# Moving 512 columns by bank halves in conv-in and the first MLP's up units, with the sums on GpSimd

## The reference, cut to what matters

```
mod = silu(c) @ ada_w[i] + ada_b[i]; sh1, sc1, gt1, sh2, sc2, gt2 = split(mod, 6)
h = modulate(rmsnorm(x, norm_g[0, 0]), sh1, sc1)
b_gate, c_gate, hv = split(h @ w_in, 3)          # w_in: 1024 x 3072, "conv-in"
x = x + gt1 * ((b_gate * causal_conv3(c_gate * hv)) @ w_out)
h = modulate(rmsnorm(x, norm_g[0, 1]), sh2, sc2)
x = x + gt2 * (square(relu(h @ w1)) @ w2)        # w1: 1024 x 4096 "up", w2 "down"
```

## Time and profile before

| what | us |
|---|---|
| median of 3 runs | 1351.02 (1350.86 to 1354.01) |
| span of the profiled execution, first to last instruction | 1350.7 |
| PE, DVE, ACT, POOL busy in the span | 1303.9, 948.4, 701.1, 128.3 |
| conv-in's units on PE | some 36 to 114 |
| first MLP on PE | some 141.5 to 332 |

### The profile page before, as it was taken

One profiled execution on the slowest core, in us unless ns is written; L12 is line 12 of the kernel. 1 busy time (PEld: TensorE's weight loads), 2 busy tenths in 40 slices (PEclk: granted clock), 3 DMA queues, 4 the chain that ended last, 5 costly groups with the idle time before them and its releaser, 6 DMA issues. The chain is left out here.

```text
span 1350.7 us, 24951 instructions
## 1 busy us (share of the span) xinstructions
PE 1303.9 (97%) x10507; PEld 1130.7 (84%) x10507; DVE 948.4 (70%) x1433; ACT 701.1 (52%) x1211; POOL 128.3 (9%) x133
## 2 busy tenths in 40 slices
PE   4999999999999999999999999999999999999997
PEld 2998888997899887788888887888888998888886
DVE  1887788976768776685556888666657677756655
ACT  2534544434467455564444648654445566644443
POOL 0000000010200864100000142000000021000000
PEclk9999999999999999999999999999999999999999
DMA  9997899995341012356665532465565544565561
GB/s 363 373 366 236 302 350 381 356 344 161 110 156 64 4 35 97 98 178 196 188 192 177 176 121 74 150 203 192 187 196 160 170 143 126 172 188 192 183 197 51
DMA packets 177559, 256.90 MB, mean 190 GB/s; under 512 B 10472, under 2 KB 122536, under 8 KB 177448
## 3 DMA queue, kind: packets, MB, share of 16 engines
q1 hardware_dynamic: 177448, 255.31, 57.0%
HBM read 254.25 MB, written 1.05 MB: 189 GB/s over the span
## 5 line engine op out<-in xcount | busy, mean ns | idle before, releaser
L1507 DVE TENSOR_TENSOR w_lo<-stage,w_hi 128x1024 fp32r<-128x1024 f32 (+1 forms) x372 | 447.3, 1238 | 160.4 <-ACT w_hi L882 160.0
L882 ACT ACTIVATE w_hi<-stage 128x1024 fp32r<-128x1024 f32 (+1 forms) x378 | 379.9, 1049 | 211.7 <-PE acc L2311 191.9
L2309 PE MATMUL acc<-w_hi,z_hi 128*128 128x512 f32 x640 | 252.7, 395 | 1.6 <-DVE z_lo L1956 1.6
L2311 PE MATMUL acc<-w_hi,z_lo 128*128 128x512 f32 x640 | 249.4, 390 | 0.0
L2310 PE MATMUL acc<-w_lo,z_hi 128*128 128x512 f32 x640 | 249.2, 389 | 0.0
L2252 PE MATMUL un<-h_both,w_hi 128*128 128x256 f32 x736 | 214.9, 292 | 1.8 <-POOL w_lo L853 1.1
L2253 PE MATMUL un<-h_both,w_hi 128*128 128x256 f32 x736 | 208.8, 284 | 0.0
L2254 PE MATMUL un<-h_both,w_lo 128*128 128x256 f32 x736 | 208.8, 284 | 0.0
L2252 PEld LDWEIGHTS un<-h_both,w_hi 128*128 128x128 f32 x736 | 141.6, 192 | 9.5 <-issue 5.4
L2309 PEld LDWEIGHTS acc<-w_hi,z_hi 128*128 128x128 f32 x640 | 120.1, 188 | 27.8 <-issue 3.9
L2253 PEld LDWEIGHTS un<-h_both,w_hi 128*128 128x128 f32 x736 | 141.7, 193 | 1.2 <-issue 0.7
(11 more groups left out here) (393 smaller groups left out, 1885.1 us busy)
## 6 DMA issues: line engine op xcount, KB each, us to landing
stage<-in_mlp_w SPq DMA_DIRECT2D x64, 1024.0 KB
ada_buf<-in_ada_w SPq DMA_DIRECT2D x48, 1024.0 KB, 11.1
stage<-in_w_up SPq DMA_DIRECT2D x32, 1024.0 KB
stage<-in_w_down SPq DMA_DIRECT2D x32, 1024.0 KB
stage<-in_conv_w_in SPq DMA_DIRECT2D x12, 1024.0 KB
stage<-in_rw_w_rkv SPq DMA_DIRECT2D x12, 1024.0 KB
stage<-in_w_in_a SPq DMA_DIRECT2D x8, 1024.0 KB
stage<-in_w_kv_b SPq DMA_DIRECT2D x8, 1024.0 KB
```

Of the source, the lines that this page charges most:

```text
L882: A_(w_hi[u % 2][:, half, 0:n], stage[u % NSTAGE][:, half, 0:n], ACT.Copy).then_inc(hi_made, 1)
L1507: V.tensor_tensor(w_lo[u % 2][:, half, 0:n], stage[u % NSTAGE][:, half, 0:n], w_hi[u % 2][:, half, 0:n].bitcast(F32), ALU.subtract).then_i ...
L2309: MM(y, z_hi[:, kt, q], wh[:, i, :], start=(first and kt == 0), stop=False, skip_group_check=True)
L2311: ins = MM(y, z_lo[:, kt, q], wh[:, i, :], start=False, stop=(last and kt == KT - 1), skip_group_check=True)
```

## The change

Conv-in's 12 units and the first MLP's 16 up units (`HALF_UNITS`) are made by `half_unit`: W_hi moves both parts of h, 512 columns, and W_lo moves h_hi, 256 columns. The first output half goes to bank un[0] in full, then the second to bank un[1]. Each bank then holds two partial results side by side. ACT copies each bank as it stands to an SBUF tile `halves`; POOL adds the two parts. In the MLP POOL also makes the maximum with 0 and the product zf. DVE no longer makes the square; in conv-in it takes the last four sums from SBUF in place of PSUM. ACT's copy of the next unit's first half is queued behind z_hi. The lora_mu products move behind POOL's last three squares, `halves` takes the place of sq, one gate row moves to the place of the middle constants, and their load is queued behind SP's wait for x. Some waits are rewritten as links.

```diff
+        HALF_UNITS = [*range(U_CONV_IN, U_CONV_IN + 12), *(U_MLP[0] + 2 * UPD * g + j for g in range(GROUPS) for j in range(UPD))]
@@ SP
                 if u == U_MLP[0] + 8:
+                    sp.wait_ge(sem("x_ready"), x_done(N_MLP0))
                     sp.dma_start(const[1][:], A["const_table"][:, CONST_AT[1]:CONST_AT[2]]).then_inc(sem("const_mid_in"), 16)
-                    sp.wait_ge(sem("x_ready"), x_done(N_MLP0))
@@ POOL
+            for i in range(len(HALF_UNITS)):
+                pool.wait_ge(un_free, freed(half_use(i)))
+                both = halves[i % 2]
...
+                if i < 12:
+                    G.tensor_tensor(to, both[:, :, 0, :], both[:, :, 1, :], ALU.add).then_inc(sum_made, 1)
+                else:
+                    k = Z_MLP0 + i - 12
+                    link(G.tensor_tensor(to, both[:, :, 0, :], both[:, :, 1, :], ALU.add))
+                    link(G.tensor_scalar(both[:, :, 1, :], to, 0.0, None, ALU.max))
+                    pool.wait_ge(z_lo_made, k - 1)
+                    G.tensor_tensor(zf[k % 2][:], both[:, :, 1, :], to, ALU.mult).then_inc(zf_ready, 1)
+                if i >= len(HALF_UNITS) - 3:
+                    lora_scale(*LORA_COLS[i - len(HALF_UNITS)])
@@ ACT
+            def copy_half(i, m):
+                if m:
+                    act.wait_ge(unit_done, HALF_UNITS[i] + 1)
+                else:
+                    act.wait_ge(half_done, i + 1)
+                if 2 <= i < 14:
+                    act.wait_ge(sum_made, i - 1)
+                A_(halves[i % 2][:, m, :, :], un[m][:, :, :], ACT.Copy).then_inc(un_free if m else half_free, 1)
@@ ACT, mlp
-                            A_(relu_b[j % 2][:], un[(v + j) % 2][:], ACT.Relu).then_inc(relu_ready, 1)
+                            if j == 0:
+                                copy_half(12 + UPD * g, 0)
+                            copy_half(12 + UPD * g + j, 1)
...
                         if m == 0:
+                            if j < UPD - 1:
+                                copy_half(12 + UPD * g + j + 1, 0)
                             copy_set(COPIED_AT.get(S_MLP + 2 * UPD * g + j))
@@ DVE, mlp
-                            V.scalar_tensor_tensor(out=zf[k % 2][:], in0=un[(v + j) % 2][:], scalar=0.0, in1=relu_b[j % 2][:],
-                                                   op0=ALU.max, op1=ALU.mult).then_inc(zf_ready, 1)
@@ DVE, conv
-                    V.tensor_tensor(u_pad[:, t0:t0 + 2, 2:PADT], un[(V_CONV + j) % 2][:], tmp[:, t0:t0 + 2, :], ALU.mult).then_inc(un_free, 1)
+                    link(V.tensor_tensor(u_pad[:, t0:t0 + 2, 2:PADT], halves[j % 2][:, :, 0, :], tmp[:, t0:t0 + 2, :], ALU.mult))
@@ PE
+            def half_unit(i, ready=None):
+                def rows(kt, m):
+                    MM(un[m][:, :, :], wh[:, kt, c], h_both[:, kt, :, :], start=(kt == 0), stop=False, skip_group_check=True)
+                    ins = MM(un[m][:, 0, :], wl[:, kt, c], h_hi[:, kt, :], start=False, stop=(kt == KT - 1), skip_group_check=True)
...
+                together = KT - 2 if ready is not None else 0
+                if i:
+                    pe.wait_ge(half_free, i)
...
+                for m in range(2):
+                    if m:
+                        pe.wait_ge(un_free, freed(half_use(i) - 1))
+                    for kt in range(together, KT):
...
+                        rows(kt, m)
```

More of the change, by code:

```diff
@@ L202, in build @@
         zf = [at(f"zf{i}", [P, 2, SEQ], scr_off + 12 * 1024 + 2048 * i) for i in range(2)]
-        relu_b = [at(f"relu{i}", [P, 2, SEQ], scr_off + 16 * 1024 + 2048 * i) for i in range(2)]
+        halves = [at(f"halves{i}", [P, 2, 2, SEQ], sq_off + 4096 * i) for i in range(2)]
         up_sum = [at(f"up_sum{i}", [P, 2, SEQ], scr_off + 16 * 1024 + 2048 * i) for i in range(2)]
@@ L2278, in unit, with low_parts @@
                     ins.then_inc(unit_done, 1)
+            def half_unit(i, ready=None):
+                u = HALF_UNITS[i]
+                wh, wl = w_hi[u % 2], w_lo[u % 2]
+                def rows(kt, m):
+                    c = slice(P * m, P * m + P)
+                    MM(un[m][:, :, :], wh[:, kt, c], h_both[:, kt, :, :], start=(kt == 0), stop=False, skip_group_check=True)
+                    ins = MM(un[m][:, 0, :], wl[:, kt, c], h_hi[:, kt, :], start=False, stop=(kt == KT - 1), skip_group_check=True)
+                    if kt == KT - 1:
+                        ins.then_inc(unit_done if m else half_done, 1)
+                def low_parts(kt):
+                    if kt % (KT // 2) == 0:
+                        pe.wait_ge(lo_made, 2 * u + kt // (KT // 2) + 1)
+                together = KT - 2 if ready is not None else 0
+                if i:
+                    pe.wait_ge(half_free, i)
+                if together:
+                    pe.wait_ge(un_free, freed(half_use(i) - 1))
+                for kt in range(together):
+                    low_parts(kt)
+                    ready(kt)
+                    for m in range(2):
+                        rows(kt, m)
+                for m in range(2):
+                    if m:
+                        pe.wait_ge(un_free, freed(half_use(i) - 1))
+                    for kt in range(together, KT):
+                        if m == 0:
+                            low_parts(kt)
+                            if ready is not None:
+                                ready(kt)
+                        rows(kt, m)
             def up_unit(u, pair, ready=None):
@@ L2463, in mlp @@
                         if m == 0:
-                            free_bank(v + UPD * g + j)
-                            unit(u + 2 * UPD * g + j, un[(v + j) % 2], (h_hi, h_lo), ready)
+                            half_unit(12 + UPD * g + j, ready)
                             ada_piece(S_MLP + 2 * UPD * g + j)
@@ L2500, in _ @@
             for j in range(12):
-                free_bank(V_CONV + j)
-                unit(U_CONV_IN + j, un[(V_CONV + j) % 2], (h_hi, h_lo), h_ready(N_CONV) if j == 0 else None)
+                half_unit(j, h_ready(N_CONV) if j == 0 else None)
                 ada_piece(S_CONV + j)
```

52 lines of the change are left out of this document (25 added, 27 removed).

## The result

| | before | after |
|---|---|---|
| median, same chip | 1350.94 us (1350.80 to 1354.01) | 1379.8 us (1377.96 to 1382.29) |
| span of the profiled execution | 1350.7 | 1379.4 |
| conv-in and conv-out, to the first sum of the MLP's norm | 138.38 | 143.28 |
| first MLP, from there to the first sum of the next norm | 196.24 | 221.20 |
| DVE, ACT, POOL busy in the span | 948.4, 701.1, 128.3 | 960.8, 717.7, 227.8 |

The ratio is 1.0206, with a 95% interval of 1.0187 to 1.0225: slower by 28 to 29 us. Of the 28.7 us between the two spans conv-in and conv-out give 4.9 and the MLP 25.0; the rest of the kernel is 1.2 us shorter. The two norm sums (DVE, norm_st) are the marks for the stages in everything that follows. Each mark comes from one trace.

A forecast was written before the change was run, and what follows sets the result against it. PE's own instructions were taken to bound the kernel. MLP +21.1 us (20.4 stalls, 3.6 weighing, less 2.9) and conv-in +0.3 made +21.4 on 1351.0: 1372.4 us, range 1354 to 1386.

The forecast's parts named there:

- The gain, -5.0: Conv-in and MLP: 28 units each 0.18 us shorter on PE, -5.0 us, 2.2 in conv-in and 2.9 in the MLP.
- no gain in pitch: Rival for PE's units: alternating 512 and 256 columns take 0.36 us, adding 5 us; within the range, no separate chance given.
- The maximum, 0.74: MLP: POOL's one-input maximum with 0 over 512 columns takes 0.74 us, between rows of 0.20 and 1.05.
- The bounds that hang on the maximum, -6.5 or +3.7: MLP: a maximum of 0.20 or 1.05 us moves twelve stalls by 0.5 or 0.3, the total by -6.5 or +3.7.
- The chain: MLP: POOL's operations alternate with w_lo halves, then z_hi, so ACT's next first-half copy ends at T+6.98, bank needed at T+5.53.
- The exclusion: POOL and DVE instructions with both inputs in SBUF exclude each other: 1.06 us per addition, 1.14 per w_lo half, 1.25 per weighing.
- Waits at the banks, 2.8 us per group: MLP: PE stands 1.4 us for the bank in the third and fourth units of each group, 2.8 us per group.
- The down unit, 2.3 per group: MLP: PE stands 2.3 us per group in the first down matrix, waiting for w_lo's second half.
- Weighing, +3.6: MLP: in nine of sixteen up units DVE's weighing excludes POOL for 2.5 us more, costing 0.4 each, +3.6 us.
- The clock: Rival, MLP: PE's standing makes its clock fall, five falls for +8 us, 1381 and up to 1390; chance 0.10.
- Conv-in, +0.3: Conv-in: 0.4 us at the first bank copy and 2.1 at the last z_lo, less 2.2 of gain, +0.3 us.
- Costed at nothing: The const table's later load, moved lora_mu products, no-ops, rewritten waits and DMA add nothing; lora_mu up to 1 us without room.

The follow-up runs named there:

- run 4: Changed kernel, but in the first MLP VectorE makes sum and square from ScalarE's copies and GpSimd none; conv-in as changed: 1352.61 us, ratio 1.0007.
- run 6: Run 4's MLP (VectorE makes sum and square), with conv-in as in the kernel before the change: 1350.45 us, ratio 0.9987.
- run 11: Run 8 with GpSimd's maximum and product also made each unit, of constants into tiles that nothing reads: 1377.66 us, ratio 1.0192.
- run 10: Changed kernel with GpSimd's second operation in four forms in turn: maximum into zf, multiplication by 1.0, plain copy, maximum as it is: 1379.2 us.
- run 5: Changed kernel with two unread PE products ahead of the first down unit of the MLP's groups 0, 1 and 2: 1377.51 us, ratio 1.0184.
- run 3: Changed kernel with only conv-in by halves, the first MLP as in the kernel before: 1355.68 us, ratio 1.0024.
- run 8: Changed kernel with ACT's next copy ahead of z_hi, GpSimd making only the MLP's sum and VectorE the squared Relu: 1356.31 us, ratio 1.0033.
- run 7: Run 4 with only conv-in's first eight units by halves, its last four as before the change: 1351.11 us, ratio 0.9987.
- run 9: Run 6 with GpSimd's sum, maximum and product made each unit of constants, into tiles that nothing reads: 1378.82 us, ratio 1.0201.
- run 2: Changed kernel without the MLP's maximum (Relu left out); POOL multiplies the sum by itself: 1358.47 us, ratio 1.0042.
- run 12: Run 8 with 18 one-column GpSimd operations between its sum and the signal to VectorE: 1431.84 us, ratio 1.0588.
- run 1: Changed kernel with ACT copying the next unit's first half ahead of z_hi in the first MLP: 1370.41 us, ratio 1.0129.

## Why the prediction was right, point by point

The sign and the likeliest mechanism held, and 1379.8 us lies within the range, 7.4 above the forecast. That it came so near is in part luck: several terms were wrong and cancel. By its steps:

- **The gain, -5.0.** Mis-sized. I took 0.69 us for two halves from a place with the same products in another order; in this order a half takes 0.353 and a unit gains 0.10 us, not 0.18. 28 x 0.10 = 2.8. Runs 4 and 6 confirm it: 1.4 us in 16 units. The rival "no gain in pitch" was half right: +2.2 us.
- **The maximum, 0.74.** Too short by a factor of two, and outside both bounds: 1.35 us behind a wait for DVE, 1.48 to 1.50 where DVE is free (run 11). I had bounded it by a copy of 8 elements and by a product with a broadcast operand, and took a missing second stream for a saving. The Trainium skill (GPSIMD Engine Reference, section 4.1: one-input work "roughly line-rate") gave 0.64; the trace does not bear that out for the maximum; run 10's copy, 0.47 behind its wait, stays within it.
- **The bounds that hang on the maximum, -6.5 or +3.7.** Wrong in kind. With a copy of 0.47 in its place the chain was as long (run 10): where w_lo's second half follows, the product waits for it either way.
- **The chain.** The right length, and most of its steps. Measured from T = 155.26 (the second of the two copies), with my figures in brackets: the sum starts at T+0.68 (0.63), w_lo's first half ends at T+3.05 (2.90), the maximum at T+4.40 (3.44), w_lo's second half at T+4.60 (4.58), the product at T+5.77 (5.78); z_hi starts at T+5.80 (5.78) and the next copy at T+6.34 (6.38). That the end fits in spite of the maximum is two errors of opposite sign: it took longer than I thought, and it held w_lo's second half by 0.41 us where I had it stand for the whole.
- **The exclusion.** Right, and the step that decides. POOL's instructions waited for DVE's to end (the maximum 0.99 us, a sum up to 1.17), and a sum took up to 2.33 us in place of 1.27 to 1.30; DVE's w_lo took 1418 ns in the mean of 56 rows in place of 1235. Too strict in one direction only: the maximum does not hold DVE for its whole length. The Trainium skill (SBUF — State Buffer, "Who interferes with whom") lets the first hold the pair for its whole instruction; the trace agrees where DVE is first, and where POOL is first with two tiles, but not for the maximum, which held a half of w_lo 0.41 of its 1.35 us.
- **Waits at the banks, 2.8 us per group.** Released by ACT's copy, in the third and fourth units, as said; 0.2 to 1.7 each where I had 1.4. They sum to 6.1 us in six, against 11.2 in eight; two more of 0.86, in the third unit of groups 2 and 3, are released by ACT's copy of the modulation row behind the same queue.
- **The down unit, 2.3 per group.** 2.38, 2.38 and 2.36 in three groups, released by w_lo: the best-hit term. In the fourth it was 1.48, for the modulation.
- **Weighing, +3.6.** Not tried by itself. The MLP's waits are 18.6 us, 20.5 more than before from start to start, in place of the 24.0 that banks, down units and weighing summed to.
- **The clock.** The largest thing left out of the sum. I had it as a rival with 0.10; it came together with the likeliest case rather than in its place. Four falls more than before are 6.8 us; run 5 speaks for two of them coming from PE's standing. That and the likeliest case were one case, since what makes PE stand can make the clock fall.
- **Conv-in, +0.3.** It was +4.9, and +2.8 to +3.9 in four traces of the same conv-in that have no fall of the clock there (runs 3, 8, 10, 11). The 2.1 us at its end came, as 2.01, seen first at the modulation's row (122.61) because that stands ahead of z_lo in DVE's queue. Missed were 2.10 us at 105.11, where ACT's copy of the modulation row is queued behind a z_hi that waits for POOL's sum; 1.7 us of clock behind the second wait; and 1.0 of the gain. Run 7 shows that most of it (3.6 of 4.1 us) hangs on the last four units. I had costed DVE's lateness there, but not what ACT carries behind z_hi.
- **Costed at nothing.** Constants, lora_mu and no-ops: none of their tiles shows in PE's waits up to 375 us. Right as far as the trace shows it.
- **The signs.** All four for "right" came: POOL busy 105.8 us between 42 and 350 (I had some 70), w_lo longer than 1.22, PE's waits at the third and fourth units, and those at the down product. One reading was off: the earlier trace rows have DVE busy in 81 to 87% of the time, not from 74.

The MLP as measured: 20.5 us of standing from start to start (21.7 - 1.2), 5.1 for three falls of the clock, less 1.6 for the gain, are 24.0 of the 25.0; the last 1.0 is open. Against my +21.1 that is 3.5 less standing, 5.1 of clock that I had left out, 1.3 of gain that did not come and the 1.0.

## What to carry to other kernels

Before moving work to an idle GpSimd, ask what VectorE does in the same microseconds, and not only who waits for the result: run 9 lost 28.9 us to results that nobody reads. Count a chain through GpSimd in turns, not in the lengths of its instructions: a turn here waited wherever VectorE was at an instruction with two inputs in SBUF, and a copy in place of a maximum changed nothing. Before a long row is taken for a price, look at what the other engine was doing when it started. A sum in the chain of a tile that is needed at once (conv-in's last four units) costs what stands behind it in every queue, ScalarE's side jobs included; the same sum into a tile needed later cost little (run 7). If PE must stand for two microseconds now and then, add the falls of its clock to the bill, or give it unread products to do.

## What the runs showed of the hardware that I had not expected

- A GpSimd instruction that starts while VectorE runs one with two inputs in SBUF takes what that has left and then a fixed time of its own: 1.35 us for a 128x512 fp32 tile with a constant (1.34 to 1.35 in all 16 maxima of the changed kernel), 1.12 to 1.20 for two tiles, 0.90 for a tile with itself (run 2), 0.47 for a copy (run 10). With VectorE free it is 1.48 to 1.50 for the constant and, at most times, 1.27 to 1.31 for two tiles.
- The other way round, a VectorE instruction that starts during a two-tile one of GpSimd's stands for the rest of it, less 0.13 to 0.21 us (w_lo 0.13 to 0.14). During one with a constant, or a copy, it stands 0.40 to 0.41 us at most times.
- GpSimd operations of one column take 0.29 us each with their links, 17 in 4.88 us, and do not lengthen VectorE's w_lo (1219 ns against 1218); short instructions are no cheap delay there.
- 0.44 us of VectorE time is lost per microsecond of busy GpSimd in run 9 over run 6: (204.4 - 169.3) / (85.1 - 5.2). In run 11 over run 8 it is 27.3 / 58.7 = 0.47. It is no constant: in run 12 over run 8 it is 9.9 / 80.5 = 0.12, and run 2 has 23.9 us less of GpSimd than run 1 with the same VectorE time.
- Products of 512 and 256 columns in turn have a pitch of 0.355 us per pair, barely under three of 256 (0.36).
- PE's clock fell for 3.4 us behind single waits of 2.0 to 2.4 us four times in the changed kernel. Where two of these waits were cut to 0.9 and 1.0 us by unread products it did not fall; behind other waits of 2.0 to 3.2 us it did not fall either.
